# VectorE's order and a head's order of keys and queries in the attention loop of a two-layer hybrid mixer step

## The reference, cut to what matters

```python
q = (_rmsnorm(q_lat, w['q_norm_g']) @ w['w_q_up']).reshape(B, L, N_HEADS, QK_NOPE + QK_ROPE)
...
kv = (ckv_all @ w['w_kv_up']).reshape(B, Lk, N_HEADS, QK_NOPE + V_DIM)
k_nope, v = kv[..., :QK_NOPE], kv[..., QK_NOPE:]
...
        s = jnp.einsum('bqhd,bkhd->bhqk', qblk, k, preferred_element_type=jnp.float32) * scale
        p = jax.nn.softmax(s, axis=-1).astype(v.dtype)
        return jnp.einsum('bhqk,bkhd->bqhd', p, v)
```

## Time and profile before

| | before |
|---|---|
| time, median of 3 runs (lowest to highest) | 2216.41 us (2216.18 to 2216.81) |
| time of the profiled execution | 2216.42 us |
| its span, first to last instruction | 2214.3 us |
| busy PE / DVE / ACT / POOL | 96% / 49% / 40% / 33% |
| mean granted TensorE clock | 0.994 |
| attention loop, layer 0 and layer 1 | about 303.7 to 617.7 and 1382.8 to 1697.4 us |

### The profile page before, as it was taken

How to read it: one execution, slowest core, us unless ns; L and a number is a source line. 1 busy time by engine, 2 the same in 40 slices (tenths; PEclk the granted TensorE clock), 3 DMA queues, 4 the chain that set the end, 5 groups by cost and what they waited for, 6 DMA issues and landing times.

```text
span 2214.3 us, 36107 instructions
## 1 busy us (share of the span) xinstructions
PE 2133.8 (96%) x13185; PEld 2033.8 (92%) x13185; DVE 1074.1 (49%) x2775; ACT 887.3 (40%) x2223; POOL 732.0 (33%) x656
## 2 busy tenths in 40 slices
PE   6999999999999999999999999999999999999997
PEld 4899888888899999999989998888888999999997
DVE  2441268888764668663162314888886111120213
ACT  2421267787831212113152214787787122111312
POOL 1323133443422234333441312343443123433242
PEclk9999999999999999999999999999999999999999
DMA  9811000000353333324255100000014111111232
GB/s 280 266 30 31 26 1 1 2 1 2 121 156 86 93 84 101 81 64 144 73 194 163 40 1 25 2 1 1 2 35 171 48 37 48 43 46 39 63 124 86
DMA packets 194622, 155.68 MB, mean 70 GB/s; under 512 B 8636, under 2 KB 186000, under 8 KB 193424
## 3 DMA queue, kind: packets, MB, share of 16 engines
q1 hardware_dynamic: 194448, 153.38, 22.6%
HBM read 124.89 MB, written 28.48 MB: 69 GB/s over the span
## 4 chain that ended last, share of the span: by engine, by line
PE 85%; DVE 6%; ACT 4%; issue 3%; DMA 1%; POOL 0%; SPq 0%; DVEq 0%; POOLq 0%; ACTq 0%
PE ps L1625 24%; PE ps L1627 23%; PE ps L1626 23%; PE ps L1817 5%; PE ps L1842 3%; PE ps L1843 2%; DVE partmax L1467 1%; DVE probsT L1480 1%; ACT probs L834 1%; PE ps L1635 1%; ACT probsT L850 1%; DMA raw<-in_w_mod 1%; PE ps L1860 1%; DVE xn_high L1226 1%; PE ps L1821 1%
## 5 line engine op out<-in xcount | busy, mean ns | idle before, releaser
L1625 PE MATMUL ps<-xn_high,split_br 128*128 128x384 f32 x1584 | 531.7, 336 | 0.0
L1627 PE MATMUL ps<-xn_high,split_br 128*128 128x384 f32 x1584 | 529.4, 334 | 0.0
L1626 PE MATMUL ps<-xn_low,split_br 128*128 128x384 f32 x1584 | 529.3, 334 | 0.0
L967 ACT ACTIVATE sigmoids<-ps 128x384 f32<-128x384 f32 x144 | 70.4, 492 | 613.1 <-PE ps L1627 613.1
L1009 POOL TENSOR_TENSOR split_br<-raw,split_br 128x1024 fp32r<-128x1024 f32 x82 | 198.0, 2416 | 320.4 <-ACT split_br L695 320.4
L1626 PEld LDWEIGHTS ps<-xn_low,split_br 128*128 128x128 f32 x1584 | 297.5, 188 | 0.0
L1625 PEld LDWEIGHTS ps<-xn_high,split_br 128*128 128x128 f32 x1584 | 297.4, 188 | 0.0
L1627 PEld LDWEIGHTS ps<-xn_high,split_br 128*128 128x128 f32 x1584 | 297.4, 188 | 0.0
L1480 DVE TENSOR_TENSOR probsT<-ps,probsT 128x384 fp32r<-128x384 f32 x384 | 213.3, 556 | 74.9 <-ACT sum_inv_rows L857 36.4
L834 ACT ACTIVATE probs<-ps,negmax 128x384 f32<-128x384 f32 (+1 forms) x400 | 229.7, 575 | 38.2 <-DVE negmax L1473 37.6
L850 ACT ACTIVATE probsT<-ps 128x384 fp32r<-128x384 f32 x384 | 188.8, 492 | 67.7 <-PE ps L1817 40.3
(11 more groups left out here) (228 smaller groups left out, 4156.8 us busy)
## 6 DMA issues: line engine op xcount, KB each, us to landing
raw<-in_w_in SPq DMA_DIRECT2D x74, 512.0 KB, 4.0
raw<-in_w_mod SPq DMA_DIRECT2D x48, 512.0 KB, 5.3
park_high<-xn_high SPq DMA_DIRECT2D x6, 1536.0 KB, 6.2
park_low<-xn_low SPq DMA_DIRECT2D x6, 1536.0 KB, 10.6
xn_high<-park_high SPq DMA_DIRECT2D x2, 4608.0 KB, 15.9
rows<-in_x_sample SPq DMA_DIRECT2D x16, 512.0 KB, 6.9
raw<-in_w_out SPq DMA_DIRECT2D x16, 512.0 KB, 6.6
rows_mid<-rows SPq DMA_DIRECT2D x9, 512.0 KB, 2.6
```

The source lines that it names most:

```text
L1625: mm(out, wh, xh, start=first, stop=False)
L1626: mm(out, wh, xl, start=False, stop=False)
L1627: return mm(out, wl, xh, start=False, stop=last)
```

## The change

Three edits, all in the attention loop:

1. The last partial maximum of tile s+1 and its negated maximum leave the start of step s+1 and go to the end of step s: the maximum ahead of the third `turned_low`, the negation behind it. In the step before a context block (j = 7) both now come ahead of `head_weights`.
2. `unmix` moves from ahead of the first `turned_low` to behind the first partial maximum.
3. The pieces of the next head are made keys first (j = 1, 2, 3), queries after (j = 4, 5, 6); the waits on the shared working copies follow that order.

```diff
-DVE_STEP = (("beside", 0), ("unmix", 0), ("low", 0), ("sum", 0), ("max", 0), ("low", 1),
-            ("max", 1), ("low", 2))
+DVE_STEP = (("beside", 0), ("low", 0), ("sum", 0), ("max", 0), ("unmix", 0), ("low", 1),
+            ("max", 1), ("last", 0), ("low", 2), ("neg", 0))
...
-        return [("qk"[n // 3], h + 1, n % 3)]
+        return [("kq"[n // 3], h + 1, n % 3)]
...
-            filled(sp, l, "attn", attn[("k", HEADS - 1, 2)])
+            filled(sp, l, "attn", attn[("q", HEADS - 1, 2)])
...
-                    act.wait_ge(S("q_low"), (l * HEADS + h) * 3 + (3 if h else 0))
+                    act.wait_ge(S("q_low"), (l * HEADS + h) * 3)
...
-                    dve.wait_ge(S("k_low"), (l * HEADS + h) * 3 + (0 if h else 3))
+                    dve.wait_ge(S("k_low"), (l * HEADS + h) * 3 + 3)
...
-            maxes(0, 0)
-            maxes(0, 1)
+            for c in range(3):
+                maxes(0, c)
+            negmaxes(0)
             for s in range(STEPS):
-                if s < TILES:
-                    maxes(s, parts(s) - 1)
-                    negmaxes(s)
                 for what, c in DVE_STEP:
...
+                    if what == "last" and s + 1 < TILES:
+                        maxes(s + 1, parts(s + 1) - 1)
+                    if what == "neg" and s + 1 < TILES:
+                        negmaxes(s + 1)
```

## The result

The changed kernel takes 2295.22 us (median of 4 runs, 2293.29 to 2299.3) against 2216.61 in the runs beside it: a ratio of 1.0357, interval 1.0339 to 1.0375, 78.6 us slower. The forecast was 2285, its range 2245 to 2305.

What follows compares the result with a forecast made beforehand. PE bounds the kernel, busy for 96% of the span. Late mixings, bank waits and head changes add 34.2 us a layer, 68 for two, to 2216.41: 2285 us, range 2245 to 2305.

Steps and rivals of the forecast that it cites:

- The sum's place: j2, j3, j5: `unmix` behind maximum 0 makes mixings about 1.0 us later after T0 (the step's turn 0); j7 0.7.
- The sum for a head: The steps from T0 of j1 to the next head's take 44.64 us against 40.12, 4.5 more.
- Maximum and keys: Low 2 comes 0.2 us later, so its bank holds the next T0; the keys' 0.73 wait goes, lost at j8.
- even heads and head 7: Heads 1 to 5 priced alike at 4.5 us more each, head 6 at 3.8, head 7 at 5 for four late mixings.
- 23 late mixings a layer: Term of the range: late mixings in the attention loop, each uncertain by 0.2, 9 us.
- The clock: Attention loop: granted clock taken as unchanged at 1.00, the upper level of 2.4 GHz, since PE stays mostly busy.
- a rival of 0.05: More, 2330 us: the clock falls in parts, or waits for the bank and `unmix` build on one another; chance 0.05.
- the prediction's own sign of being wrong: Low 0 nearer to T0, mixings still at + 1.8, or granted clock in the loops below 1.00.
- Faster: Rival, 2188 us: PE's waits in j7, j8 and j0 go in 14 changes of heads, 28 us; chance 0.05.
- Half the loss: Rival, 2250 us: PE wins part of each gap back through small waits behind the mixing, 34 us lost; chance 0.13.
- No change: Rival, 2216 us: the later `unmix` costs what the transitions between heads return; chance 0.03.

Runs made afterwards that it cites:

- the sum first: Changed kernel with the mixings' sum put back ahead of the first low part; third maximum and keys stay as changed: 2209.92 us.
- the last run with ACT's copies moved: Changed kernel, sum ahead of low 0, head weights at ends of j0 and j3, value copies later, gate splits at ends of j3 and j5: 2210.52 us.
- the run with the late sum and ACT's copies moved: Changed kernel with even heads' value copies behind the next step's first turned copy and head 7's gate splits at ends of j3 and j5: 2296.61 us.
- the smaller dose: Changed kernel with the mixings' sum directly behind the first low part, ahead of the sums and the first maximum: 2249.38 us.

## Why the prediction was right

**The sum's place: right, as cause and as mechanism.** Put back, it returns 85.3 us; alone, it costs 86.5. Mixings are at T0 + 3.02, 2.67, 2.94 and 2.48 in j2, j3, j5 and j7, and the one of j0 10.99 behind T0 of j7, where the prediction had 3.05, 2.65, 2.77, 2.30 and 11.06.

**The sum for a head: right for odd heads.** j1 4.78 (4.73 forecast), j2 5.65 (5.53), j3 5.61 (5.50), j4 4.74 (4.73), j5 and j6 10.99 (11.05), j7 to j0 13.04 (13.10): 44.81 against 44.64. One agreement is luck, two errors that cancel: against the sum first j5 and j6 lose 1.3 and not 1.0, but with keys first and the sum first they take 9.69 and not the 10.0 that the row of before gave. T0 of j3 waits for low 2 (0.86) and turn 2 of j8 for the part behind the head weights (0.47), as forecast.

**Maximum and keys: right that neither pays for the loss.** The prediction gave the maximum a bank wait that lengthens steps. It makes no delay of its own: without the late sum it costs nothing (2216.07), and on top of it, queries first, at most some 3 us (2306.51 against 2303.22, whose intervals overlap).

**What was mis-sized: even heads and head 7.** In the profiled execution the span grew by 83.0 where the sum had 68.4. The two loops, from first score to last mixing, are 42.0 and 39.1 longer, not some 34 each; the other 2.0 lie outside them. Cut as the sum is, from T0 of j1 to T0 of j1, the odd heads took 28.3 more (27.0 forecast) and the two heads 0 2.4 each (2.9); the six even heads took 33.2 (25.6 forecast, four of 4.5 and two of 3.8), head 7 with the steps behind it 14.9 (10). Of the 7.6 too little in even heads, the clock has some 3.9: in the table above five of them lie 0.4 to 1.1 above the one whose clock stayed at 1.00 (46.00). That leaves 3.7, 0.6 a head, for ACT's key and value copies. The prediction named these copies, at 0.8 a head, in its range and not in its sum. In head 7 it is the gate split, which it did not name: moving the two splits takes 3.5 and 1.9 us off it, the larger figure where the clock had fallen as well. Against the median, 2295.2, the forecast is 10 us short and inside its range. The range itself was drawn too narrow at one term: it counts 23 late mixings a layer, and PE waits at 37.

**The clock: the step that was wrong.** The forecast took it as unchanged from rows with waits up to 0.7 us, and kept the lower level for a rival of 0.05. In the changed kernel five even heads and head 7 of layer 0 show 0.96, and the end of head 7 in both layers 0.91, part of each at the lower level of 1.2 GHz. So the prediction's own sign of being wrong, a clock below 1.00 in the loops, came up, and that rival came true for some 4 us in even heads and 1.6 in head 7 of layer 0 (42.08 against 40.51), of 79; what it took at the ends of head 7 no run shows. The time lies in the range all the same, because what can be read of the clock is some 5.5 us. The Trainium skill, "TensorE: Matmul & The Clock Gate", section "A second HAM failure mode: psum-queue depth-cycling", tells of a kernel in which PE is briefly idle between groups of products and the clock goes back and forth between both levels. The trace of those heads agrees with it; the odd heads, with six waits of 0.8 to 1.3 in each, stayed at 1.00 and do not show it.

**The rivals.** Faster needed low 0 near T0; it stayed at T0 + 1.15. Half the loss needed small waits behind the mixing to give time back; a single late mixing in j5 lost 1.2 to 1.3, more than the 1.0 that its delay was priced at, so nothing was given back. No change needed the transitions to return the loss; j7 to j0 take 13.04, more than the 12.44 of before.

## What to carry to other kernels

An operation that an idle engine does while it waits for something is free only in that place: moved behind the thing waited for, it becomes a link of the chain, and its price is the whole wait. Before moving one, look at what is tied to the critical engine's own last step (here low 0, 1.1 us behind T0) and keep everything that the critical engine needs next ahead of that. And price each kind of step by itself: the heads with an extra copy in the queue in front lost 5.0 us where the plain ones lost 4.5, and up to 6.4 where the clock fell as well.

## What the runs showed of the hardware

The granted clock fell, for a few us each time, mostly at a single wait of PE of 1.2 to 2.4 us, but in the last run with ACT's copies moved also behind two waits of 0.74 and 0.92 close together. Behind the wait of 2.31 in head 2 of the changed kernel, a turn took 0.86, and the next T0, 3.2 us later, 0.52 again. It is not the same each time: in the changed kernel all six even heads have this wait at 2.31 to 2.33, and the clock fell in five; in the run with the late sum and ACT's copies moved six heads have waits of 1.26 and 2.4, and it fell in two. What it cost differs too: a head in which it fell took 0.4 to 1.1 us more in the changed kernel, 1.5 with ACT's copies moved, 2.1 in the smaller dose, and 0.3 or nothing in the last run with ACT's copies moved (41.4 to 41.7, against 41.4 at 1.00). The spread of the runs does not show it: it is 6 us for the changed kernel against 0.75 for the kernel before beside it, but the kernel before spreads by 4.5 to 8 us beside the other runs. What decides between two heads of one schedule was not found.
